# Modulation by quarters, early parts of the first group, and three smaller moves in a two-block kernel

## What is computed

```
mod = silu(c) @ ada_w + ada_b              # 2048 x 6144
shift, scale, gate = split(mod, 3)
h = rms_norm(x, norm_g) * (1 + scale) + shift
proj = h @ w_in                            # the first long product; 2048 x N_IN
...
lb = cumsum(softmax(hgrn_lb_logits))[0]    # lower bound of the forget gate
q, k, qi, ki = rope(...)                   # needs cos and sin of the angles
```

## Time and profile before

| | us |
|---|---|
| median of 3 runs | 2105.76 |
| lowest and highest | 2101.82 and 2106.73 |
| the profiled execution | 2106.29 |
| its span, first to last instruction | 2104.5 |
| PE busy in the span | 2058.0 (98%) |
| DVE, ACT, POOL busy | 1302.7, 927.1, 383.0 |

### The profile page before, as it was taken

How to read it: one execution, slowest core, us unless ns; L and a number is a source line. 1 busy time by engine, 2 the same in 40 slices (tenths; PEclk the granted TensorE clock), 3 DMA queues, 4 the chain that set the end, 5 groups by cost and what they waited for, 6 DMA issues and landing times.

```text
span 2104.5 us, 23568 instructions
## 1 busy us (share of the span) xinstructions
PE 2058.0 (98%) x9245; PEld 1623.4 (77%) x9245; DVE 1302.7 (62%) x1651; ACT 927.1 (44%) x1224; POOL 383.0 (18%) x588
## 2 busy tenths in 40 slices
PE   6989999999999999999999999999999999999999
PEld 1268787777887888786788888888888888878887
DVE  4857667798666678865765666554544544444443
ACT  1165523455654544354454434554444444433332
POOL 0000002999999950000000000000000000000000
PEclk9999989999999999999999999999999999999999
DMA  9967557555565675554435555555555555546554
GB/s 353 344 236 249 199 185 220 180 171 164 171 213 196 200 231 180 160 163 130 138 129 186 187 198 180 180 194 187 191 188 186 194 186 194 194 166 199 186 195 160
DMA packets 205683, 408.47 MB, mean 194 GB/s; under 512 B 10826, under 2 KB 12163, under 8 KB 204931
## 3 DMA queue, kind: packets, MB, share of 16 engines
q1 hardware_dynamic: 190480, 376.07, 54.1%
q10 hardware_dynamic: 13332, 24.40, 3.4%
q0 software_dynamic: 1760, 6.49, 1.5%
HBM read 404.83 MB, written 2.10 MB: 193 GB/s over the span
## 4 chain that ended last, share of the span: by engine, by line
PE 91%; DVE 6%; DMA 2%; issue 1%; ACT 0%; ACTq 0%; SPq 0%; DVEq 0%
PE ps L430 81%; PE pm L511 6%; DMA raw<-in_ada_w 2%; DVE raw_lo L408 1%; PE ps L511 1%; PE pm L523 1%; DVE mod_part L1151 1%; PE pm L575 1%; PE pm L888 0%; DVE gate L1182 0%; DVE xtmp L1351 0%; DVE sc_i L1268 0%; DMA rows_b<-in_hgrn_norm_g 0%; DVE proj L1328 0%; PE pm L710 0%
## 5 line engine op out<-in xcount | busy, mean ns | idle before, releaser
L408 DVE TENSOR_TENSOR raw_lo<-raw,w_hi 128x1024 fp32r<-128x1024 f32 (+1 forms) x648 | 799.9, 1238 | 597.6 <-ACT w_hi L399 589.0
L399 ACT ACTIVATE w_hi<-raw 128x1024 fp32r<-128x1024 f32 (+1 forms) x648 | 680.1, 1050 | 821.0 <-PE ps L430 796.3
L430 PE MATMUL ps<-w_hi,h_hi 128*128 128x512 f32 (+1 forms) x2336 | 941.3, 403 | 12.5 <-DVE raw_lo L408 6.4
L430 PE MATMUL ps<-w_hi,h_lo 128*128 128x512 f32 (+1 forms) x2336 | 912.5, 391 | 0.0
L430 PE MATMUL ps<-raw_lo,h_hi 128*128 128x512 f32 (+1 forms) x2336 | 911.2, 390 | 0.0
L430 PEld LDWEIGHTS ps<-w_hi,h_hi 128*128 128x128 f32 x2336 | 442.8, 190 | 117.3 <-issue 13.0
L430 PEld LDWEIGHTS ps<-raw_lo,h_hi 128*128 128x128 f32 x2336 | 443.3, 190 | 93.3 <-issue 7.7
L430 PEld LDWEIGHTS ps<-w_hi,h_lo 128*128 128x128 f32 x2336 | 442.2, 189 | 93.4
L2265 POOL TENSOR_TENSOR proj<-proj 128x128 f32<-128x128 f32 x264 | 177.8, 679 | 12.9
L2265 POOL TENSOR_TENSOR proj<-proj,w1T 128x128 f32<-128x128 f32 x165 | 102.8, 631 | 11.4 <-DMA proj<-in_z 4.2
L430 PE MATMUL ps<-w_hi,hid_hi 128*128 128x512 f32 x256 | 100.6, 393 | 2.0 <-DVE raw_lo L408 2.0
(11 more groups left out here) (308 smaller groups left out, 1183.5 us busy)
## 6 DMA issues: line engine op xcount, KB each, us to landing
raw<-in_w_in SPq DMA_DIRECT2D x140, 1024.0 KB, 5.2
raw<-in_w_ffn_gate SPq DMA_DIRECT2D x44, 1024.0 KB, 5.2
raw<-in_w_ffn_up SPq DMA_DIRECT2D x44, 1024.0 KB, 5.2
raw<-in_w_ffn_down SPq DMA_DIRECT2D x44, 1024.0 KB, 5.2
raw<-in_ada_w SPq DMA_DIRECT2D x32, 1024.0 KB, 7.7
raw<-in_w_out SPq DMA_DIRECT2D x32, 1024.0 KB, 5.2
proj<-in_ada_w ACTq DMA_DIRECT2D x16, 1024.0 KB, 5.3
raw<-in_w_br_hyena SPq DMA_DIRECT2D x8, 1024.0 KB, 5.2
```

The lines of the kernel that those rows point to most:

```text
L399: nc.scalar.activation(w_hi[:, p % HRING, :, 0:gm.width(j)], raw[:, k % RING, e:e + HT, 0:gm.width(j)], ACT.Copy).then_inc(hi_done, 1)
L408: nc.vector.tensor_tensor(raw_lo[:, k % RING, e:e + HT, 0:gm.width(j)], raw[:, k % RING, e:e + HT, 0:gm.width(j)], w_hi[:, p % HRING, :, 0 ...
L430: mm = nc.tensor.matmul(ps[pair][:, t, 0:gm.width(j)], l[:, tok], r[:, i, 0:gm.width(j)], start=(k == 0 and q == 0), stop=(k == kt - 1 and ...
```

## The change

1. Modulation goes by quarters. The order of the groups becomes shift 0, scale 0, shift 1, scale 1 and so on. After each pair, its quarter of the columns is turned and added (`columns_of`), and in the next even group ACT and DVE make four of the sixteen tiles of `h` from it. All turns of `hbuf` now lie in groups 2 to 5 of the front, and ACT copies them to `h1_raw`.
2. The loads of `ada_w` get four buffers of their own in `proj` (`ada_raw`), with `ada_landed`. The first two chunks of `w_in` are issued ahead of the last group of `ada_w`.
3. PE takes chunk 0 and three rows of chunk 2 (two in the last group). DVE takes chunk 1, the rest of chunk 2, and chunk 3.
4. The parts 0 and 1 of group 0 (`EARLY = 2`) are multiplied before the last row of the modulation is complete.
5. The constants on ACT's queue are issued after the root of the row norms, not right after x.
6. The lower bound (but for a maximum and two subtractions) stands beside parts 9 to 15, the angles beside part 16 and later. The gate row's pieces begin at part 24 (before: 12).
7. Index products take four at a time, the halves of the partitions in turn. The taps alternate halves.

```diff
-ADA_PE = 1
+PE_C2 = 3
+EARLY = 2
+LB_AT = 9
-GATE_AT = [12 + 22 * i // 5 for i in range(4 * ADA_GATE)]
+GATE_AT = [24 + 54 * i // 15 for i in range(4 * ADA_GATE)]
...
+        ada_raw = [proj[:, 1, o:o + CK * GW].rearrange("p (k n) -> p k n", k=CK) for o in (A_Q, A_V, R_Q, R_I)]
...
         def ada_free(sp, g, c):
 
-            if c != 1:
-                sp.wait_ge(ada_used, 3 * (g - 1) + {0: 1, 2: 2, 3: 3}[c])
-            if c % 2:
-                sp.wait_ge(mod_parts, 2 * (g - 1) + 1 + c // 2)
+            if c % 2 == 0:
+                sp.wait_ge(ada_used, 2 * (g - 1) + 1 + c // 2)
+            if c:
+                sp.wait_ge(mod_parts, 3 * (g - 1) + c)
...
             for g in range(n_ada):
+                q = g // 2 - 1
+                if 2 <= g < 6:
...
+                mods = bank(pe, ("mods", q), "v") if q >= 0 and g % 2 == 0 else None
+                sums = bank(pe, ("mod", g), "a")
+                row_sums(g, 0, CK, sums)
+                if mods is not None:
+                    turn_modulation(q, mods)
+                row_sums(g, 2, pe_rows(g), sums)
+                if g == n_ada - 1:
+                    for n in range(EARLY):
+                        first_part(n)
+                pe.wait_ge(mod_parts, 3 * g + 3)
+                mm(sums[0:1, :], ones[:, 0:1], mod_part[:, g % 2], start=False, stop=True).then_inc(filled, 1)
+            first_part(EARLY)
...
-                        part = slice(IDX_D * (j % 2), IDX_D * (j % 2) + IDX_D)
                         for q in range(2):
-                            m = mm(b[:, q * SEQ:q * SEQ + nk], qiT[part, j // 2 * 2 + q, t * P:t * P + P], kiT[part, 0:nk])
-                        m.then_inc(filled, 1)
+                            for r in range(2):
+                                part = slice(IDX_D * r, IDX_D * r + IDX_D)
+                                m = mm(b[r][:, q * SEQ:q * SEQ + nk], qiT[part, j + q, t * P:t * P + P], kiT[part, 0:nk])
...
-                    t, n = i // 4, i % 4
+                    t, n = i % TT, i // TT
...
+                yield 2.0
+                dve.wait_ge(sig("lb_in"), 16)
+                link(v.tensor_tensor(lb_tmp, lb[:, 0], lb[:, 1], ALU.max))
...
             act.wait_ge(sig("x_in"), 16)
             for j in range(D // GW):
                 squares("h1", j)
...
+                read_row(g)
+                if g == 0:
                     root("h1")
+                    constants_in()
...
             for g in range(n_ada):
+                o = D * (g % 2) + GW * (g // 2)
                 for c in range(RING):
+                    if g:
+                        ada_free(sp, g, c)
+                    sp.dma_start(ada_raw[c], ada_v[:, CK * c:CK * c + CK, o:o + GW]).then_inc(ada_landed[c], 16)
+                if g == n_ada - 2:
+                    for c in range(2):
+                        load(sp, g_in, 0, c)
```

More of the change, by code:

```diff
@@ L334, in build @@
         landed = [sem(f"landed{i}") for i in range(RING)]
+        ada_landed = [sem(f"ada_landed{i}") for i in range(RING)]
         ada_used = sem("ada_used")
@@ L419, in multiply_group @@
                     before(n)
[L420 to L432, removed]
+                multiply_part(pe, gm, j, n, stat)
                 if beside is not None:
-                    beside.step(p)
+                    beside.step(gm.part(j, n))
         def multiply(pe, gm, stat, before=None, beside=None):
@@ L555, in _, with row_sums @@
[L555 to L558, removed]
+            def row_sums(g, c, n, b):
+                pe.wait_ge(ada_landed[c], 16 * (g + 1))
+                for k in range(n):
+                    m = mm(b[0:1, :], c_sig[:, CK * c + k:CK * c + k + 1], ada_raw[c][:, k], start=(c == 0 and k == 0), stop=False)
+                m.then_inc(ada_used, 1)
@@ L560, in _ @@
+            first_part(EARLY)
+            q = n_ada // 2 - 1
+            turn_modulation(q, bank(pe, ("mods", q), "v"))
+            for n in range(EARLY + 1, g_in.parts):
+                first_part(n)
             class Chains:
@@ new lines, in _ @@
+                    if g == n_ada - 1 and c == 2:
+                        for n in range(EARLY):
+                            low(dve, g_in, 0, n)
+                    early.step(g, 3.0 if g < 2 else 1.2)
+            early.rest()
+            for n in range(EARLY, HRING):
+                low(dve, g_in, 0, n)
+            columns_of(n_ada // 2 - 1)
+            low(dve, g_in, 0, HRING)
+            low_of_first(KT // 2 - 2)
+            low(dve, g_in, 0, HRING + 1)
+            low_of_first(KT // 2 - 1)
@@ L1173, in gate_row @@
+            for n in range(HRING + 2, g_in.parts):
+                low(dve, g_in, 0, n)
+            angles = Spare(rotation_angles())
             def gate_row():
@@ L1418, in _ @@
             gate_sum = Spare(gate_sums())
+            groups(g_in, (1, 2, 3), None, ((chain, 1e9), (angles, 1.5), (gate_work, 1.0)))
+            assert angles.over
             beside = ((chain, 1e9), (gate_sum, 1e9), (gate_work, 1.0), (head_work, 1.2))
-            groups(g_in, range(1, g_in.groups), None, beside)
+            groups(g_in, range(4, g_in.groups), None, beside)
             assert gate_work.over and head_work.over and gate_sum.over
```

296 lines of the change are left out of this document (161 added, 135 removed).

## The result

The changed kernel takes 2112.10 us (median of 9 runs, 2107.15 to 2113.78), the kernel before on the same chip 2106.73 (9 runs): a ratio of 1.0031, interval 1.0016 to 1.0047. The change is slower by some 6.5 us by this ratio (5.4 between the two medians). The profiled execution spans 2107.6 us where before it was 2104.5.

A forecast was written before the change was run, and what follows sets the result against it. PE was taken to bound the kernel (91% of the chain). Front +0.5, DVE waits +2 and row halves -5 sum to -2.5 us: 2106.3 becomes 2103.8, less 0.5 above the median 2103 us; range 2090 to 2118 (8 in 10).

The forecast's parts named there:

- Step 1: Front, group 1: DVE waits 16 us (11 to 21) for hgrn_lb_logits, issued behind 12 us of constants.
- S: Instant when hgrn_lb_logits lands in the front: 47 us, with bounds of 42 and 52.
- Step 2: Front after the wait: even groups take 14.4 us, odd 8.2, so group 0 ends at S + 95, 142 us.
- E(1): End of PE's product of ones for group 1 in the front, put at S + 5.5 us.
- step 3: PE's clock in the front: two cold places add 4.5 us, group 0 ends at 146.5 against 146.0, +0.5 us.
- the bound of 155: Sign for the front: the prediction falls if group 0 ends before 138 or after 155 us.
- E(6): End of PE's product of ones for group 6 in the front, put at S + 63.9 us.
- The second rival: Front: PE falls to the lower clock level in every pair, +16 us, so 2118 or so; chance 0.24.
- Step 4: Parts 8 to 31: moved work makes DVE 96% busy (64.6 of 67 us), +2 us of waits (0 to 6).
- Step 5: Index products and taps: row halves overlap, four products in 5 slots instead of 8, -5 us (0 to -8.6).

The follow-up runs named there:

- e1: The changed kernel, with DVE's maximum and subtractions of the lower bound and their wait moved from group 1 to group 3: 2103.97 us, 0.9998.
- e2: The changed kernel, with the transfer of hgrn_lb_logits issued right behind x, ahead of the squares and the other constants: 2102.65 us, 0.9997.
- e3: The kernel before with the row halves alone (index products four at a time in turn, taps in turn): 2099.57 us, 0.9978.
- e8: The kernel before with only the order of the taps' products changed, so that the row halves alternate: 2101.59 us, 0.9992.
- e6: e5 with three products of 512 float32 columns added behind chunk 2 of groups 2, 4 and 6, into an unread bank: 2099.89 us, 0.9975.
- e5: e2 with the constants' transfers taken apart, three issued behind each group's row copy from group 1 on: 2100.66 us, 0.9987.
- e7: e5 with the first two chunks of w_in issued inside group 7's ada_w loads instead of ahead of them: 2101.76 us, 0.9992.
- e10: e6 with e7's edit and a third of the share for the angles, carried on beside groups 4 and up: 2096.66 us, 0.9970.
- e9: The changed kernel with both orders of the row halves put back, so front and moved DVE work stand alone: 2117.53 us, 1.0062.
- e4: The changed kernel with EARLY = 0, no part of group 0 ahead of the last row: 2114.10 us, 1.0048.
- e11: e10 with the index products' order of the kernel before put back, the taps' order still changed: 2096.04 us, 0.9965.

## Why the prediction was wrong

It said 2103 us and "the same", with 0.27 for slower. The measured ratio lies above no change, and the 2112 us lie in the stated range, near its slow end.

**Step 1, the new wait: right.** S = 47 was 44.9, the 12 us of issues were 12.0, the landing took 4.85 us instead of 7, and DVE waited 12.85 us for 16. That the wait decides was right too: e1 and e2 take the loss back. Missed was that ACT's copy of row 1 stands behind the same issues. The prediction named what is queued behind the wait on DVE, but not what is queued on ACT behind the constants themselves.

**Step 2, the relay of groups: the step that failed.** E(1) was S + 6.3 for 5.5. The even groups took 16.8, 14.9 and 15.4 us for 14.4, 14.4 and 13.2 (+5.1 in all), the odd ones 10.0 and 9.5 for 8.2 (+3.1), group 7 17.4 for 12.3 (+5.1). These 14.1 us, less the 4.5 that step 3 had set aside, less 2.1 for the earlier S and with 1.1 more at the end (20.9 for 19.8), make the miss: group 0 ended 8.7 us late, at 155.2 instead of 146.5, outside the bound of 155 that the prediction set itself, if by little. The scatter of the front seen in e3 and e8 (up to 3.5 us) is less than half of it.

What failed is that the sum let the loads of `ada_w` run wholly beside the relay. Their sum a pair (22.6 us) was exactly that of the relay, and group 7 had no term for them at all, though two chunks of `w_in` had been put ahead of its four. As an estimate, six chunks of 1 MiB at the 372 GB/s of the earlier trace rows take 16.9 us, where the sum had 12.3 and the trace has 17.4. DVE had its first chunk of group 7 4.9 us after E(6), where the sum had it at once, chunk 0 of group 6 came 1.75 us after PE was ready, and DVE had chunk 3 of groups 3 and 5 0.6 and 1.2 us after the sum's instants: together about 8.5 of the 14.1 us.

```profile
104.23 3.59 PE L525 MATMUL pm<-proj,c_sig 128*1 128x512 f32 x8 [1.75 <-DMA proj<-in_ada_w]
```
```profile
122.72 0.49 DVE L1199 TENSOR_SCALAR mod_part<-proj,c_sig 128x512 f32<-128x512 f32 x1 [5.70 <-DMA proj<-in_ada_w]
```

The sum of such waits says nothing by itself: from 20 to 140 us DVE waited 26.5 us for `ada_w`, 8 times, in the changed kernel and in before alike. It is their places that count. This account is read from the rows; no run made the loads smaller or gave them more buffers. Some 0.8 us more are a wait of PE for ACT's copy in group 4. The rest, about 5 us, is PE's clock.

**Step 3, the clock: right in what falls, near in size.** In the changed kernel the rows behind the pauses did run at the lower level. In group 2 the turns of `hbuf` took 1.97 us for 1.2, chunk 0 4.62 for 3.6 and the product with ones 1.87 for 1.0, and in group 3 14 records took 7.34 (above) where e6 shows 6.17:

```profile
51.19 1.97 PE L580 MATMUL pm<-ident,hbuf 128*128 128x128 f32 x8
53.08 4.62 PE L525 MATMUL pm<-proj,c_sig 128*1 128x512 f32 x8
```

In all the distances hold some 5 us of it, against the 4.5 counted. The second rival counted 16 us on top, in all pairs, and the time it gave, 2118, was the nearest on that side. But the pauses of 3.9 us in groups 2, 4 and 6 didn't bring the fall each time: the product behind them took 1.87, 1.08 and 1.57 us. Nor is it sure that the 5 us would be won at the upper level. In group 3 DVE had finished at 75.47 and PE's product came at 77.03, yet DVE then stood until 82.55 for its next chunk; and in e6 the upper level in groups 3 and 5 ends the front where it ended in e5.

**Step 4, DVE beside later parts: right here, by luck.** PE waited for `raw_lo` 1.0 us in the 67 us behind group 0, for +2 (0 to 6). DVE was busy 60.07 of them (90%, forecast 96%). The same work cost 3.2 us in e1, e2, e5, e6 and e7, and thinning it (e10) took them back. In the changed kernel the distance is that of before all the same, and a stretch of lower clock is missing there that before has (0.83 from 190 to 200 us). That the one made up for the other is an argument, no run tests it.

**Step 5, the halves: -5 became -5.5, by luck.** The term was right, its parts were not. The halves run fully side by side: eight index records take 0.72 and 1.14 us where four took 0.71 and 1.13, and four of the taps 1.13 where it was 1.98. The Trainium skill ("TensorE: Matmul & The Clock Gate", the part on packing small matmuls) says that products in different row groups run concurrently, and the trace agrees. That is near half of the serial time, not the 5 slots for 8 that I took. The busy time saved is 7.3 us in the index stretch and 3.4 in the taps. Near -10 would have been right for PE alone. At the end stand -2.1 and -3.4, since in the index stretch PE then waits for DVE (e3). "Halves" should have been costed against DVE's 13.62 us of 14 in that window, which the trace of before shows.

**The sum** was +0.5 + 2 - 5 against the measured profile's +9.2 + 0 - 5.5, with a rest of -0.6. Apart from the front's term the terms held, two of them by luck.

## What to carry to other kernels

When a transfer is moved behind a chain of issues, look at everything that its queue's engine does next, not only at who waits for the data: here one chain of 12 us stopped DVE by its last transfer and PE by a copy queued behind it. Putting that transfer first (e2) brought the front's last product with ones 7.5 us ahead, and splitting the chain three by three as well (e5) another 5.2. A stage in which each turn releases the next loads must be timed by its transfers as well as by its turns, with every load counted that shares its time. Before giving an engine's room to moved work, or halving PE's work in a stretch, ask how busy the second engine is in that very stretch: what is gained ahead of it is lost in it.

## What the runs showed of the hardware

The granted clock falls to the lower level in short stretches without any wait of PE, and not in each profile at the same place. A window of before and one of e9 behind the same work, PE busy throughout, and the row just ahead of each:

```profile
930.00:940.00 10.00, 10.00 (x36) 8.35 (x37) 2.82 (x4) 1.56 (x2) 0.00 (x0) 0.69 0.21 55
```
```profile
940.00:950.00 10.00, 10.00 (x51) 8.30 (x51) 4.62 (x9) 2.12 (x2) 0.00 (x0) 1.00 0.33 107
```
```profile
926.99 4.68 PE L511 MATMUL pm<-ones,proj 128*128 128x1 f32 x32
```
```profile
937.74 3.63 PE L525 MATMUL pm<-ones,proj 128*128 128x1 f32 x32
```

In the eleven profiles that have this stretch it comes right behind these records of one column each, which count as busy. In e4 and e9 the same records take 3.63 us and no fall follows. So they come before each fall here but don't bring it every time. The fall in before at 195.8 us also stands behind 32 narrow records, those with `ind`, and the same records in the changed kernel bring none.

From the last of the taps' products to the last of `sc_pT` it is 235.1 us in before, in the changed kernel and in e3, 235.2 in e8, and 232.0 in e4 and e9, which have no such stretch: one such stretch costs 3.1 us (in e11, where it is shorter, 1.6). Another lies in the first attention steps. Here the first three steps of before and of e5 (start, us):

```profile
280.65 0.42 PE L511 MATMUL pm<-qaT,kaT 128*32 128x64 f32 x16
284.63 0.65 PE L511 MATMUL pm<-qaT,kaT 128*32 128x64 f32 x16
294.33 0.65 PE L511 MATMUL pm<-qaT,kaT 128*32 128x64 f32 x16
```
```profile
279.10 0.42 PE L525 MATMUL pm<-qaT,kaT 128*32 128x64 f32 x16
284.83 0.65 PE L525 MATMUL pm<-qaT,kaT 128*32 128x64 f32 x16
294.53 0.65 PE L525 MATMUL pm<-qaT,kaT 128*32 128x64 f32 x16
```

From the first to the second step it is 3.98 us in before and 5.73 in e5, where the level fell within the first step: this is the other 1.8 us that e5 lost. In e11 it fell later again (3.79 us to the second step; 5.83 in e10). Its first state product is 2.4 us ahead of e10's, and with 1.5 us behind the taps this is where its span is shorter, although its index stretch is 1.2 us longer. What makes it fall there in the one and not in the other was not found. The spread of 4.5 to 12 us between runs of one kernel is of the size of two to four such stretches; that they are its cause is an argument and was not shown.
